# Bias and maximum in one VectorE operation, and another order of VectorE's work inside a step, in a hybrid attention and mLSTM layer

## The reference

```python
h = rmsnorm(x, norm_pre) * (1 + scale) + shift
u = h @ w_in                      # one projection of 12,296 columns, split among all users
# branch A: differential attention, 8 heads, two softmax maps c = 0, 1
s = einsum('bqhcd,bkhcd->bhcqk', q, k) * (HD_A ** -0.5)
s = where(k_pos <= q_pos, s + bias, -inf)      # bias = -slope(h) * (q_pos - k_pos)
p = softmax(s, axis=-1)
a = p[:, :, 0] - lam * p[:, :, 1]
att = einsum('bhqk,bkhe->bqhe', a, v)
# branch B: mLSTM, 4 heads
num = inter * (q @ C) + (s @ v);  den = inter * (q @ n) + sum(s)
hm = num / maximum(abs(den), exp(-m_t))
y = (sigmoid(g_a) * (att_normed_gated @ w_br_a) + sigmoid(g_m) * (hm_normed_gated @ w_br_m)) @ w_out
x = x + gate * rmsnorm(y, norm_post)
```

## Time and profile before

| | us |
|---|---|
| median of 3 runs | 2185.51 |
| lowest, highest | 2181.76, 2190.83 |
| the profiled execution: time | 2187.54 |
| the profiled execution: span from first to last instruction | 2185.9 |
| TensorE busy | 2045.4 (94%) |
| VectorE busy | 800.1 (37%) |
| ScalarE busy | 621.5 (28%) |

### The profile page before, as it was taken

How to read it: one execution, slowest core, us unless ns; L and a number is a source line. 1 busy time by engine, 2 the same in 40 slices (tenths; PEclk the granted TensorE clock), 3 DMA queues, 4 the chain that set the end, 5 groups by cost and what they waited for, 6 DMA issues and landing times.

```text
span 2185.9 us, 37865 instructions
## 1 busy us (share of the span) xinstructions
PE 2045.4 (94%) x15108; PEld 1895.0 (87%) x15108; DVE 800.1 (37%) x1554; ACT 621.5 (28%) x1108; POOL 161.1 (7%) x281
## 2 busy tenths in 40 slices
PE   5999999988898888999999999999999999989996
PEld 3779999877787877778889999999999999989996
DVE  3455334466632224443333432222233223243334
ACT  3212222334344433322322322222222222222221
POOL 2000001000020000001321000000000000110000
PEclk8999999999999999999989999999999999999998
DMA  9772332221143331122333333343343343472222
GB/s 342 254 252 74 103 99 77 59 87 44 44 150 121 121 100 43 47 57 76 107 89 88 82 81 108 116 112 106 116 111 113 110 117 111 128 218 83 73 77 101
DMA packets 177618, 240.30 MB, mean 110 GB/s; under 512 B 14497, under 2 KB 145697, under 8 KB 175785
## 3 DMA queue, kind: packets, MB, share of 16 engines
q1 hardware_dynamic: 157472, 177.24, 28.2%
q0 software_dynamic: 17808, 61.53, 8.3%
q10 hardware_dynamic: 2242, 0.19, 0.1%
HBM read 220.02 MB, written 18.89 MB: 109 GB/s over the span
## 4 chain that ended last, share of the span: by engine, by line
PE 72%; issue 12%; DVE 9%; ACT 5%; DMA 2%; POOL 0%; DVEq 0%; ACTq 0%; POOLq 0%
PE gemm L489 60%; PE bank_a L489 4%; PE bank_s L489 3%; PE bank_o L489 3%; DVE e_map L1640 1%; DVE w_lo L1358 1%; ACT L1022 1%; ACT w_hi L1022 1%; DVE mx L1641 1%; DMA y_back<-y_scratch 1%; ACT e_map L1022 1%; PE bank_s L724 1%; DMA ada_in<-in_w_ada 1%; DVE em_b L1737 1%; PE bank_s L514 0%
## 5 line engine op out<-in xcount | busy, mean ns | idle before, releaser
L489 PE MATMUL gemm<-h_hi,w_hi 128*128 128x288 f32 x3584 | 806.8, 307 | 37.5 <-DVE z_act L1747 17.7
L489 PE MATMUL gemm<-h_hi,w_lo 128*128 128x288 f32 x3584 | 778.9, 299 | 0.0
L489 PE MATMUL gemm<-h_lo,w_hi 128*128 128x288 f32 x3584 | 778.2, 299 | 0.0
L1358 DVE TENSOR_TENSOR w_lo<-w_raw,w_hi 128x512 fp32r<-128x512 f32 x512 | 353.6, 692 | 1096.3 <-ACT w_hi L1022 1095.7
L489 PEld LDWEIGHTS gemm<-h_hi,w_hi 128*128 128x128 f32 x3584 | 587.8, 193 | 101.4 <-issue 80.2
L1022 ACT ACTIVATE w_hi<-w_raw 128x512 fp32r<-128x512 f32 x512 | 321.3, 629 | 1059.8 <-PE gemm L489 1045.1
L489 PEld LDWEIGHTS gemm<-h_lo,w_hi 128*128 128x128 f32 x3584 | 588.4, 192 | 0.0
L489 PEld LDWEIGHTS gemm<-h_hi,w_lo 128*128 128x128 f32 x3584 | 588.0, 192 | 0.0
L489 PE MATMUL gemm<-brm,w_hi 128*128 128x288 f32 x512 | 90.7, 300 | 6.6 <-DVE y_mix L1843 6.6
L489 PEld LDWEIGHTS gemm<-brm,w_hi 128*128 128x128 f32 x512 | 77.0, 193 | 6.8 <-DVE y_mix L1843 6.8
L1022 ACT ACTIVATE e_map<-e_map,nmx 128x128 f32<-128x128 f32 (+3 forms) x64 | 35.4, 554 | 118.8 <-DVE nmx L1642 118.8
(11 more groups left out here) (401 smaller groups left out, 1482.3 us busy)
## 6 DMA issues: line engine op xcount, KB each, us to landing
w_raw<-in_w_in SPq DMA_DIRECT2D x384, 256.0 KB, 2.8
ada_in<-in_w_ada SPq DMA_DIRECT2D x32, 1024.0 KB, 9.9
ada_g<-in_w_ada POOLq DMA_DIRECT2D x32, 512.0 KB, 4.8
w_raw<-in_w_out SPq DMA_DIRECT2D x64, 256.0 KB, 2.9
k_page<-in_cache_k POOLq DMA_DIRECT2D x16, 512.0 KB, 5.5
v_page<-in_cache_v POOLq DMA_DIRECT2D x16, 512.0 KB, 4.6
w_raw<-in_w_br_a SPq DMA_DIRECT2D x32, 256.0 KB, 2.8
w_raw<-in_w_br_m SPq DMA_DIRECT2D x32, 256.0 KB, 2.8
```

The source lines that it names most:

```text
L489: return nc.tensor.matmul(out, lhsT, rhs, start=start, stop=stop, skip_group_check=True)
L1358: V.tensor_tensor(w_lo[:, slot], w_raw[:, slot], w_hi[:, slot], ALU.subtract).then_inc(lo_ready, 1)
```

## The change

Three things change, all on VectorE.

1. In the attention loop, the addition of the bias and the maximum become one `tensor_tensor_reduce` for each map: it adds the bias, writes the map, and writes the row maximum. The separate reduction over both maps goes.
2. In the attention loop the order inside a step is turned round: bias and maximum of s = x-A0-1 first, then the normalisation of s = x-A0-2, then `ahead`.
3. In the two loops after it, `ahead` moves behind the attention or mLSTM work of the step (before the gating of the last step of a pair).

```diff
+LOW = -3e38
...
             for x in range(11 * NG, 16 * NG):
                 p, g = x // NG, x % NG
-                ahead(p, g)
                 if p in (11, 12) and g in (1, 2):
                     tok_v(v_att, v_smp, 2 * (p - 5) + g - 1, 2 * (p - 9) + g - 1)
...
-                s = x - A0 - 2
-                if 0 <= s < STEPS:
-                    n = (s % NT + 1) * P
-                    dve.wait_ge(sc_exp, s + 1)
-                    link(V.reciprocal(rrec[:, s % 2, :], rsum[:, s % 2, :]))
...
                 s = x - A0 - 1
                 if 0 <= s < STEPS:
...
                     for c in range(2):
-                        link(V.tensor_tensor(e_map[:, s % 2, c, 0:n], bank_s[:, c, 0:n], alibi[:, TP - n:TP], ALU.add))
-                    link(V.tensor_reduce(mx[:, s % 2, :], e_map[:, s % 2, :, 0:n], AX.X, ALU.max))
+                        link(V.tensor_tensor_reduce(e_map[:, s % 2, c, 0:n], bank_s[:, c, 0:n], alibi[:, TP - n:TP], 1.0, LOW,
+                                                    ALU.add, ALU.max, mx[:, s % 2, c:c + 1]))
                     V.tensor_scalar(nmx[:, s % 2, :], mx[:, s % 2, :], -1.0, None, ALU.mult).then_inc(sc_max, 1)
+                s = x - A0 - 2
+                if 0 <= s < STEPS:
+                    n = (s % NT + 1) * P
+                    dve.wait_ge(sc_exp, s + 1)
+                    link(V.reciprocal(rrec[:, s % 2, :], rsum[:, s % 2, :]))
+                    link(V.tensor_scalar(rrec[:, s % 2, 1:2], rrec[:, s % 2, 1:2], neglam[:, 0:1], None, ALU.mult))
+                    link(V.tensor_scalar(e_map[:, s % 2, 1, 0:n], e_map[:, s % 2, 1, 0:n], rrec[:, s % 2, 1:2], None, ALU.mult))
+                    V.scalar_tensor_tensor(e_map[:, s % 2, 0, 0:n], e_map[:, s % 2, 0, 0:n], rrec[:, s % 2, 0:1],
+                                           e_map[:, s % 2, 1, 0:n], ALU.mult, ALU.add).then_inc(a_ready, 1)
+                ahead(p, g)
 
             for x in range(16 * NG, 24 * NG):
                 p, g = x // NG, x % NG
                 c, d = x - 16 * NG, x - 20 * NG
-                ahead(p, g)
                 b = c // 4
...
                         done.then_inc(mo_cp, 1)
+                ahead(p, g)
                 if g == NG - 1 and p >= 20:
...
             for x in range(24 * NG, 28 * NG):
                 p, g = x // NG, x % NG
                 hd = p - 24
-                ahead(p, g)
...
                                     d_s[:].unsqueeze(1).to_broadcast([P, 2, NS]), ALU.mult).then_inc(sh_cp, 1)
+                ahead(p, g)
                 if g == NG - 1:
```

## The result

The changed kernel takes 2146.8 us in the median of 6 runs (2141.2 to 2152.4), against 2184.1 us before (2180.4 to 2190.8, 6 runs). The ratio is 0.9829, with a 95% interval of 0.9806 to 0.9852: 37 us faster, where 23 were forecast and 29 were the most that the range allowed. Run again on another chip the ratio was 0.9823 (0.9794 to 0.9851). The direction and the place were right and the size was too small by more than a third.

What follows compares the result with a forecast made beforehand. TensorE, 94% busy, was taken as the bound, standing still for VectorE in the attention. Gains of 22.4 and 1.5 us, less 1 for new waits, made -23 us: 2164.5 profiled, 2163 as median; range 2156 to 2178.

Steps and rivals of the forecast that it cites:

- the ring through the low part: Attention loop: negated maximum, exponentials, high part, low part, normalisation, bias, maximum wait in a circle; the low part isn't urgent.
- The order alone: Attention loop reordered without fusing: waits of 13.6 us remain, gain near 13 us, 2173; chance 0.16 shared with the dear fused pass.
- The new operation's cost: Fused bias and maximum in attention: a pass costs the addition's 0.688 us at n = 512, plus 0.15 per maximum write.
- The step's sum of 3.50 us: VectorE's attention step at n = 512, from granule start through maximum, negation and normalisation, against a granule over at 3.3.
- the 2.4 us that I left standing: Attention: TensorE still waits 0.3 us for the normalised map at n = 512 in each of 8 heads.
- The token copy: Attention: TensorE waits 3.6 us for VectorE's copy of tokens behind a low part; 1.5 us of gain forecast.
- the gating's two shifts that cancel: mLSTM: division starts 0.6 us earlier, but the low part before the gating gives it back; 0 us, bound 2.8 either side.
- B: Rival: the fused attention pass costs addition and reduction together; gain 9 us, 2176; chance 0.16 shared with reordering without fusing.
- C: Rival: fused attention operation far slower; at three times the addition the kernel is 19 us slower, 2205; chance 0.05.
- D: Rival: low parts come too late, TensorE waits for weights in the long loops; 8 to 16 us lost, 2171 to 2179; chance 0.04.
- the sum's first line: Attention: TensorE's listed waits for negated maximum and normalised map fall from 24.8 to 2.4 us, 22.4 us gained.
- 28.4 us of listed waits: Prompt attention: TensorE's waits for negated maximum (17.4 + 1.3), normalised map (6.1) and token copy (3.6), beside 28.9 us idle.

## Why the prediction was too small

Point by point, by its own steps, against the 36.5 us between the two spans.

- What bounds the kernel, and the ring through the low part: right. The order alone takes 23 us off and the fused operation alone 21.
- The new operation's cost: right for the pass (691 ns for 688), a little high for the write of the maximum (0.083 for 0.15) and for the negation, behind which the reciprocal starts after 0.08 us. The step's sum of 3.50 us was 3.15. For that reason the 2.4 us that I left standing are not there.
- The token copy: 1.7 us gained, 1.5 forecast.
- The 1 us kept back for new waits: there are none.
- The later loops at 0, the gating's two shifts that cancel: right, with a ratio of 0.9996 for these loops alone and 17.5 us of waits behind the gating.
- The rivals: B is wrong by the 691 ns. The order alone was put at 13 us inside it and brings 23. C does not happen; its price came out when forced, by luck, as said above. D does not happen: TensorE waits for no low part. The Trainium skill's advice on fusing, from VectorE: DVE Perf Modes, section Rules for kernel authors, would have left the order's gain only; here the lower cost counted, not the number of instructions, and the fused operation alone is worth 21 us.
- The step that failed is the sum's first line, "the waits that remain ... where 24.8 us stood, that is 22.4 us gained". It took the listed waits of one engine for another as the whole of what waiting costs. Three things were missing. ScalarE's late block copies, 3.0 us, left out of my rows although they hang on the same ring. The overlap of TensorE's matmuls with those in front of them, which each wait takes away, 2.9 us. The clock, 1.5 us in one step of the stretch and 1.6 us after the wait of 2.77 us at its end. With the 2.4, the 1.0 and the 0.2 above this makes 12.6 of the missing 13.5 us. The low end of the range was the listed 28.4 us and 1 us more, so the range could not hold these either.
- The agreement of 28.4 us of listed waits with 28.9 us of idle time, from which the list seemed complete, was chance. The list left out 3.5 us of waits inside the stage, ScalarE's copies among them, and took in the 2.77 us that lie behind it.

It is not settled when a wait brings the clock down. At the end of the stage the clock held after 1.64 us and fell beside 2.77. Beside a wait of 2.6 us in one step it fell in the kernel before and held in the one with the fused operation in the old order. Of the eight waits of 2.7 us in the kernel with two extra additions five had a fall within 2 us of their end and three had none. And some 1 us of the 13.5 stays unexplained.

## What to carry to other kernels

When waits of TensorE go, count more than their listed length. Here each wait also cost the overlap with the matmuls in front, 0.22 us at transposes and 0.07 us at the scores; waits of other engines in the same ring went with them; and beside some waits of 2.6 to 2.8 us, and all the waits of 4.4 us behind the gating, the clock was at half for some us. Before trusting a list of waits, add up all of it inside one stretch and hold it against the idle time of that same stretch. In a ring over three engines, look for a job that nobody waits for soon and that stands in front of one that is waited for. Here it was enough that either the low part or the normalisation left the ring, and the three orders that do so were equal. A fused addition with maximum cost 3 ns more than the addition, and 83 ns for the write, so it paid where VectorE's chain was waited for.

## What the runs showed of the hardware that was not expected

A pass that adds two fp32 tensors and keeps the row maximum takes 691 ns for 512 elements, the addition alone 688; the separate write of the maximum 83 ns. The same 1096 to 1098 matmuls of the stretch were busy for 153.2, 154.9, 156.3 and 157.1 us at full clock, depending on how many waits stood between them and in front of what: the first transpose behind a wait adds 0.33 us of busy time, and 0.11 us when it follows without one, whether the wait was 0.28 or 1.23 us long. And where four waits were cut from 4.4 to 2.6 us, the granted clock over the same 888 matmuls went from 0.94 to 0.99, worth 5.8 us beside the 7.2 us of the waits.
